# Moving operands of an fp32r matmul stream placed at other byte offsets, and a sum over partitions issued in two column parts

## The reference, cut to what matters

```python
h = _rmsnorm(x, norm_g)
z = h @ w_in                       # 1024 x 5120: q, f, i, g_a, u, g_b, m_a, m_b
o, s_new = _hgrn2_chunked(...)     # 4 heads of 128, chunks of 32
o = _rmsnorm(o, hgrn_norm_g) * silu(g_a)
y_a = o @ w_proj_a                 # 512 x 1024
mixed = einsum('btgc,gcd->btgd', _multiscale_pool(u, ...), w_pool)
y_b = (mixed * pool_scale * silu(g_b)) @ w_proj_b
merged = sigmoid(m_a) * y_a + sigmoid(m_b) * y_b
out = x + merged @ w_out           # 1024 x 1024
```

## Time and profile before

| | |
|---|---|
| runs | 1486.6, 1485.25, 1486.58 us; median 1486.58 |
| profiled execution, first to last instruction | 1483.2 us (its own time outside the profile is not given) |
| TensorE busy | 98% of the span, 8,068 instructions |
| VectorE / ScalarE / GpSimd busy | 60% / 47% / 16% |
| DMA | 121 GB/s mean |

### The profile page before, as it was taken

The page is one execution under the profiler, slowest core; times in us unless marked ns, Lnnn a source line. Parts: engine busy times, 40 slices in busy tenths (PEclk is TensorE's granted clock), DMA queues, the critical chain, the costliest instruction groups (busy, mean ns, idle before and its releaser), DMA issues.

```text
span 1483.2 us, 21725 instructions
## 1 busy us (share of the span) xinstructions
PE 1457.5 (98%) x8068; PEld 1408.5 (95%) x8068; DVE 895.4 (60%) x1513; ACT 693.1 (47%) x1021; POOL 238.8 (16%) x227
## 2 busy tenths in 40 slices
PE   6999999999999999999999999999999999999996
PEld 5999999999999999999999999999999998999996
DVE  6767644567775446667744457776445586664444
ACT  5646533454555343555543445555334454453322
POOL 1102122110121211111212120112221110130002
PEclk9999999999999999999999999999999999999998
DMA  6322443334225333332253334323533443334337
GB/s 169 104 86 86 146 161 115 112 114 146 72 91 202 118 114 110 122 124 86 86 208 115 111 114 132 104 87 115 189 122 104 139 135 114 100 112 162 114 99 89
DMA packets 53936, 179.12 MB, mean 121 GB/s; under 512 B 13888, under 2 KB 14144, under 8 KB 52160
## 3 DMA queue, kind: packets, MB, share of 16 engines
q1 hardware_dynamic: 53824, 177.64, 38.4%
HBM read 166.46 MB, written 11.16 MB: 120 GB/s over the span
## 4 chain that ended last, share of the span: by engine, by line
PE 98%; ACT 0%; DMA 0%; DVE 0%; issue 0%; SPq 0%; DVEq 0%
PE Z L402 29%; PE Z L404 28%; PE Z L403 28%; PE B L436 1%; PE B L537 1%; PE B L445 1%; PE B L497 1%; PE B L527 1%; PE B L459 1%; PE B L441 1%; PE B L502 1%; PE B L547 0%; PE B L530 0%; PE B L461 0%; DMA xin<-xT 0%; PE B L517 0%
## 5 line engine op out<-in xcount | busy, mean ns | idle before, releaser
L836 DVE TENSOR_TENSOR wlo<-wraw,whi 128x1024 fp32r<-128x1024 f32 x280 | 367.3, 1312 | 450.8 <-ACT whi L645 450.8
L402 PE MATMUL Z<-hhi,whi 128*128 128x416 f32 x1584 | 566.1, 357 | 1.3 <-issue 1.3
L404 PE MATMUL Z<-hhi,wlo 128*128 128x416 f32 x1584 | 559.3, 353 | 0.0
L403 PE MATMUL Z<-hlo,whi 128*128 128x416 f32 x1584 | 556.2, 351 | 0.0
L645 ACT ACTIVATE whi<-wraw 128x1024 fp32r<-128x1024 f32 x280 | 295.8, 1056 | 518.0 <-PE Z L404 495.2
L402 PEld LDWEIGHTS Z<-hhi,whi 128*128 128x128 f32 x1584 | 298.6, 188 | 13.4 <-issue 8.0
L403 PEld LDWEIGHTS Z<-hlo,whi 128*128 128x128 f32 x1584 | 299.3, 189 | 3.8
L404 PEld LDWEIGHTS Z<-hhi,wlo 128*128 128x128 f32 x1584 | 298.5, 188 | 3.0
L404 PE MATMUL Z<-yhi,wlo 128*128 128x416 f32 x320 | 112.9, 353 | 0.0
L402 PE MATMUL Z<-mhi,whi 128*128 128x416 f32 x320 | 112.6, 352 | 0.0
L402 PE MATMUL Z<-yhi,whi 128*128 128x416 f32 x320 | 112.1, 350 | 0.0
(11 more groups left out here) (215 smaller groups left out, 1652.0 us busy)
## 6 DMA issues: line engine op xcount, KB each, us to landing
wraw<-w_all SPq DMA_DIRECT2D x280, 512.0 KB, 3.5
xres<-xT SPq DMA_DIRECT2D x5, 1664.0 KB, 7.2
xin<-xT SPq DMA_DIRECT2D x4, 1664.0 KB, 7.5
yT<-xres SPq DMA_DIRECT2D x4, 1664.0 KB, 7.1
s<-s_in SPq DMA_DIRECT2D x4, 512.0 KB, 5.3
ss_out<-snew SPq DMA_DIRECT2D x4, 512.0 KB, 5.3
xin<-xT SPq DMA_DIRECT2D x4, 416.0 KB, 5.1
yT<-xres SPq DMA_DIRECT2D x3, 416.0 KB, 2.5
```

The costliest lines, as they stand in the source:

```text
L402: pe.matmul(out, wh, xh, start=first, stop=False)
L403: pe.matmul(out, wh, xl, start=False, stop=False)
L404: return pe.matmul(out, wl, xh, start=False, stop=final)
L836: dve.tensor_tensor(wlo[n % RING][:], wraw[n % RAW][:], whi[n % RING][:].bitcast(F32), ALU.subtract).then_inc(wlo_made, 1)
```

## The change

`region(n)` reserves n bytes and its result is not used here, so everything behind it moves. The h tiles move by 64 bytes, the y tiles by 96, the merged region and everything behind it by 160. The weights `wraw`, `whi`, `wlo` stay. `sum_squares` issues, when `final` is true, four matmuls instead of two: both over columns 0 to 383, then both over columns 384 to 415 (NG * P = 384).

```diff
         wlo = [put(f"wlo{i}", [D], F32R) for i in range(RING)]
+        region(64)
         hhi = [put(f"hhi{k}", [T], F32R) for k in range(KD)]
         hlo = [put(f"hlo{k}", [T], F32R) for k in range(KD)]
 
+        region(32)
         yhi = [put(f"yhi{k}", [T], F32R) for k in range(KD)]
         ylo = [put(f"ylo{k}", [T], F32R) for k in range(KD)]
 
+        region(64)
         r1 = region(16 * B)
...
             def sum_squares(bank, what, final=True):
 
-                pe.matmul(bank[:, 0:T], ones_r[:], sqh[:], start=True, stop=False)
-                return pe.matmul(bank[:, 0:T], ones_r[:], sql[what][:], start=False, stop=final)
+                for lo, hi in ((0, NG * P), (NG * P, T)) if final else ((0, T),):
+                    pe.matmul(bank[:, lo:hi], ones_r[:], sqh[:, lo:hi], start=True, stop=False)
+                    mm = pe.matmul(bank[:, lo:hi], ones_r[:], sql[what][:, lo:hi], start=False, stop=final)
+                return mm
```

## The result

The changed kernel took 1490.14 us (median of 7 runs, 1488.11 to 1492.32) and the kernel before, beside it on the same chip, 1485.25 us (7 runs, 1483.89 to 1487.48). The ratio is 1.0028 with a 95% interval of 1.0019 to 1.0038: slower by 0.28%, 4.9 us by the medians. The forecast was 1478.4 us and faster. The profiled execution took 1491.36 us, 1489.6 of it in the span.

What follows compares the result with a forecast made beforehand. TensorE, busy 98% of the span, was taken as the bound: 1486.6 us minus 13.7 for the offsets plus 5.5 for the sum_squares parts gives 1478.4 us, range 1463 to 1499, the forecast's own range 1470 to 1484.

Steps and rivals of the forecast that it cites:

- (a): Stream matmuls, all three operand regions: shifted starts bring 186.7 ns each instead of 188.9 or 187.8, gaining 13.7 us.
- the surplus: Each stream matmul's 14.5 to 15.6 ns above 173.3 ns, said to need full-rate columns and weight reading, and follow the address.
- (b): sum_squares in two parts: 28 final calls cost 0.19 to 0.20 us more each, 5.5 us in all.
- (c): Buffers behind the merged region move 160 bytes; DMA unchanged, other engines covered by idle time; nothing taken.
- (d): Last tile's three clock drops, 1.7 us each: one may vanish or a fourth appear, -5.2 to +1.7 us; nothing taken.
- R1: Stream offsets do nothing, only the sum_squares price of 5.5 us is left: 1492 us; chance 0.17.
- R2: Shifted stream starts stand worse, 191 ns: 15 us more plus 5.5, 1507 us; chance 0.13.
- R3: Stream gain and sum_squares price cancel: pace about 188 ns, 5.2 against 5.5 us, 1487 us; chance 0.15.
- R4: Shifted stream starts stand much better, near 184 ns: 31 us less, 5.5 more, 1461 us; chance 0.12.

Runs made afterwards that it cites:

- the other offsets: Against the kernel before: h moved 96 bytes further, y 192, merged 224, sum_squares unchanged; single run 1493.29 us, span 1491.5.

## Why the prediction was wrong

**(a) The offsets: this is the step that failed.** I put the stream at 186.7 ns, read from three starts around a `sum_squares` call, and took the difference on all 6,672 matmuls (2.2 ns on 5,832, 1.1 on 840, 13.7 us in all). The runs show 188.9 and 187.8 nearly everywhere as before, and 0.9997 (0.9988 to 1.0006) for the offsets alone: instead of 13.7 us the offsets gained 1.0 in the profile. Two things were wrong with the reading, and both could have been seen. First its size: 0.56 us over three starts is read to 0.01 us, so each distance is known to some 3 ns, and the gain that I took from it was 2.2. The rows of the output slots have the same 0.56 us for three starts (859.35 - 858.79), in the middle of a stretch whose mean is 187.8. Second its place: distances repeat over six starts, and three of the six are the short half; 562 ns in one block stand beside 572 in the next. Behind a call the trace of the kernel before says the same: by the single starts behind the one at 833.51 us, eight distances average 186.5 ns and the next seven 192.6. Reading on by fifteen starts would have shown it. The order of blocks 0, 2, 4, 6, 1, 3, 5, 7 showed the same on a larger scale, a slot at 186.6 ns followed by one at 190.0. A piece of a pattern was taken for a pace.

Behind this stood an inference that was half right: "the surplus also follows the address". The alternation does follow it. But that an address decides where in a pattern the long distance falls doesn't say that it decides the sum. Addresses moved the sum by much only within 16 bytes (17 us at 4 bytes, 13 at 8), and the kernel before and the kernel after both begin every row at a multiple of 16. Steps of 16 bytes and more moved it by 3 us at most. There was little there for the change to gain.

**What the surplus is.** I wrote that it appears only where columns are asked for at the full rate while weights are read as well. The first half holds (348 ns at the low clock). The second is not borne out: with a third of the weight columns gone the pace was 188.15. The surplus belongs to the fp32r stream; in bf16 2.5 ns are left.

**(b) The parts.** Right: 0.19 to 0.20 us a call and 5.5 us were forecast, 0.19 and 5.3 came in the change, and with the parts alone 0.20 a call and 5.4 by the medians. Also the reason was right, that the part of 32 columns is shorter than its weight load, as the two halves of 208 show with 0.075 us a call. One detail was off: I expected all of it between the L404 ahead of the call and the L459 behind it, 0.75 us; it is 0.67, and the other 0.08 are one matmul later. L521 has its 57 records (28 + 28 + 1).

**(c) Nothing moves along.** Right: TensorE waits for the same four things, 15.7 us against 15.2, and the 0.2 us by which the norm comes later is covered on every engine.

**(d) The clock.** A fourth drop appeared in the profiled execution, as the bound had allowed (1.7 us each). In the profiles of the offsets alone and of the parts alone there were three. So it is in the profiled time of 1491.36 us. Whether it is in the other runs no trace shows; their mean granted clock is 0.990 in one of them, as in the profiled one, and 0.992 to 0.994 in five.

**The rivals.** R1, offsets that do nothing, came out: 1486.6 + 5.5 = 1492 us forecast, 1490.1 measured, 1.4 of the difference because the kernel before ran at 1485.25 this time. I gave it 0.17, against 0.55 for a pace between 184 and 187.8 or better. The reason that I gave for it was right, but the rows that I named didn't show it: slots 27 to 44 read h and y, slots 50 to 55 read merged, so their operands and addresses are not the same. What shows it is the loop. Slots 1 and 2 have the same lines, operands and addresses in each tile, and the kernel before runs their 48 matmuls in 9.02 us in the second tile and in 9.07 us in the third, 187.8 and 188.9 ns each. The first start of slot 1 and of slot 3 in the two tiles:

```profile
309.75 0.35 PE L402 MATMUL Z<-hhi,whi 128*128 128x416 f32 x1
...
318.77 0.35 PE L402 MATMUL Z<-hhi,whi 128*128 128x416 f32 x1
...
597.09 0.35 PE L402 MATMUL Z<-hhi,whi 128*128 128x416 f32 x1
...
606.16 0.35 PE L402 MATMUL Z<-hhi,whi 128*128 128x416 f32 x1
```

So something other than the address decides between them here; in the output slots an address did, as the other offsets showed. The Trainium skill's page "SBUF — State Buffer" led to the same figure by its section "SBUF: two separate sides", and the price of 4 bytes shows that this conclusion was nearly right for this change and not in general: that TensorE waits for no other engine in SBUF, as the page has it, doesn't keep it from being slowed by its own address. R2 (191 ns, 1507 us) did not come; but it is what an offset of 4 bytes on one operand does, 193.3 ns. R3's pace of about 188 in the slots that ran at 188.9 was there in one slot of three only (188.2). R4 did not come.

**What stays open.** Why the fp32r stream has two paces 1.1 ns apart; what takes an operand to a pace between or beside them in some slots (188.2 in h with the change's offsets, 188.0 at 16 bytes, 188.9 in merged at 224); whether the surplus comes from the bytes of the moving operand, those of the weights or the arithmetic of fp32r; what makes the issue gap at the boundary between tiles 0.6 us in one kernel and 2.2 in another.

## What to carry to other kernels

A pace is read over whole periods of the work and from many starts: 447 in a window settle 0.4 ns, three starts with times of 0.01 us settle 3 ns, and the first starts of two slots, 24 matmuls apart, settle 0.4 ns slot by slot. Before an alternation in a trace is called a cost, add it up over its period; the sum may not depend on what moves it. For an fp32r stream at full clock, begin each row on a multiple of 16 bytes (17 us of 1483 were at stake here), expect little of coarser alignment (3 us at most here), and don't cut off a part of a matmul that is shorter than its weight load.

## What was not expected of the hardware

- A 416-column matmul with 128 weight columns costs 188.9 or 187.8 ns in fp32r and 175.83 ns in bf16 at the same clock of 2.4 GHz; halving the weight columns of two in three changes the 188.9 by 0.7 ns.
- A moving operand that begins 4 bytes past a multiple of 16 costs 4.4 ns more a matmul than the 188.9 before, 8 bytes past it 3.3 ns, and 16 bytes none.
- The same instructions on the same addresses run at 187.8 ns in one tile and at 188.9 in another, for two whole slots. Many slot means lie 1.1 ns apart (187.8, 188.9, 190.0, and 192.2, 193.3), but not all (188.0, 188.2, 189.2, 189.5).
- Of two 32-column parts with 128 weight columns each behind long matmuls, the first holds the next start up by only 26 ns (661.01 - 660.99 in the rounded rows), the second by 112 (661.12 - 661.01), and the matmul behind them comes to pay another 80.
